# A two-layer hybrid encoder trunk: the order of the first loads, products and transposes

## Chip, cores and metric

The kernel runs on one core of one Trainium2 chip. The metric is the device time of one execution in microseconds; three runs of the kernel before are given by their median. Besides, one execution was profiled; all rows below come from it.

## Reference

The input `x` has 512 positions of 1024 features. Layer 0 mixes positions by windowed attention (16 query heads and 2 key and value heads of 64, chunks of 64 positions, a window of two chunks, a learned sink per head, key and query normalised over the head and partly rotated). Layer 1 mixes them by retention with 4 heads. Each layer then has a gated MLP with 2816 hidden features and a causal depthwise convolution of width 3. What the change touches is the beginning of layer 0:

```python
h = rmsnorm(x, norm1_g[0])
qkv = h @ w_qkv                      # 1024 -> 1024 queries, 128 keys, 128 values
q, k = rmsnorm(q, q_gain), rmsnorm(k, k_gain)   # over each head of 64
q, k = rotary(q), rotary(k)                     # first 16 of 64
p = softmax over the window and the sink of (q @ k.T) / 8
x = x + (p @ v) @ w_o
```

## The kernel before

Everything is float32 and is multiplied exactly enough by a split: each factor is a high part in fp32r and a rest, and a product is three matmuls (`mm3`, L1055: high by high, high by rest, rest by high). The input stands transposed in `x`, eight tiles of 128 features by 512 positions. ScalarE writes the high part of a weight or of a hidden tile (L287, L291), VectorE subtracts it to get the rest (L538, L543), and TensorE consumes both. Weights pass through two slots, `raw`, `w_hi` and `w_lo` with 2048 columns each. A pair of slots is a unit of work with a number (`PAIR_KV` 0, `PAIR_Q` 1 and 2, `PAIR_WO` 3 and 4, and so on); SyncE issues the load of a slot when VectorE has finished with its raw weights (`w_lo_ok`), ScalarE rewrites the high part when TensorE has finished with it (`w_used`), and TensorE waits for the rest (`unit`, L1067).

All five engines run programs that are written out by hand, each in a fixed order, and meet by semaphores. At the beginning:

- SyncE (L238) issues the first key and value load (four of the eight k, 1024 columns, slot 0), x tiles 0 to 4, the second load (slot 1), x tiles 5 to 7, and then the four query loads of 1 MB.
- ScalarE (L309 on) copies the first load in two halves, makes the high parts of x tiles 0 to 4, copies the second load, makes tiles 5 to 7, squares x tiles 0 to 3 (L302), copies the first query unit, squares tiles 4 to 7 and copies the second unit.
- VectorE (L557 on) follows it: two halves of the weights' rest, the hidden rests, the second load's rest behind tile 4; then it adds the squares up (L572, L575) with the first query unit's rest behind the third add; then the variance (L551) and the second unit's rest.
- TensorE (L1088 on) does for each of the two loads four position tiles with four k each, 128 by 256 columns: 96 matmuls into banks 0 to 3. Then come the four query units (`for cb ... for s`, L1139), each with four position tiles of 12 matmuls with 512 columns. Items are numbered n: 0 to 3 are the key and value tiles, 4 to 7 the tiles of the first 512 query columns (complete at the end of the second unit), 8 to 11 those of the rest. Ahead of tile 1 of the first unit, `columns` (L1070) multiplies the sum of squares by a column of ones into bank 6. Ahead of tile 2 it waits for the variance. Behind tile 2 of the second unit the two key heads are turned (`turn_in(0)`, `turn_in(1)`, L1101, transposes of the normalised and rotated keys). In the third unit, tiles 2 and 3 write over the banks of the turned keys and wait until these are copied out (`tp_ok`). Behind tile 0 of the fourth unit the first query heads are turned (`turn_in(2)` to `(5)`); that needs the rotations of items up to 7 (`qrot_ok` 8).
- An item passes through this chain: ScalarE squares it (`q_square`, L327, up to one item ahead of VectorE's sums), VectorE sums it over heads and scales (`q_var`), POOL takes the root (L933), VectorE normalises (L599), POOL rotates it in four steps (L945, L947, L949, L952) and copies keys (L955). ScalarE copies turned keys out in six pieces a head (`turned_out`, L335); it does this for head 0 behind the square of item 6, for head 1 behind that of item 7, and then copies the fourth query unit's weights. VectorE has that unit's rest between item 5's normalisation and item 7's sums, and the first output weights' rest behind item 7.
- POOL sets up constants, takes the root of the variance (L919) and serves the items, later the probabilities (L990).

The heads follow in a chain of their own over all four engines up to TensorE's first output product, and from there the kernel is the two MLPs and the retention, whose loops the change doesn't touch.

## Time and profile before

| what | us |
|---|---|
| median of three runs | 1292.45 (1292.0 to 1293.49) |
| the profiled execution | 1293.06 |
| its span, first to last instruction | 1291.2 |
| TensorE matmul, busy | 1269.8 |
| VectorE, busy | 697.9 |
| ScalarE, busy | 476.3 |
| POOL, busy | 202.0 |

The time of an execution is a little longer than the span of its instructions. In rows of a timeline the first number is the start in us from the start of the span, the second the length in us (of all, where x is over 1); then come engine, line of the kernel, operation, output and inputs with their sizes, the count, and in brackets how long the engine had been idle and who is taken to have ended that. TensorE's matmuls overlap, so the pace is the distance of their starts. The releaser is inferred, and where a wait is for several semaphores the name can be wrong: TensorE's first product is put down to a POOL clear, but waits also for the first hidden rest.

### The profile page before, as it was taken

The page shows a single profiled execution, that of the slowest core. Times are in us where ns is not written, and L with a number is a line of the kernel's source. Part 1 is how long each engine was busy: PE and PEld are TensorE (multiplying, and loading weights), DVE is VectorE, ACT ScalarE, POOL GpSimd, SP SyncE. Part 2 cuts the span into 40 slices and gives each one's busy share as a digit, 9 for nine tenths or more (in the row PEclk, how much of TensorE's full clock was granted, in tenths as well). Part 3 has the DMA queues.
Part 4 walks back from the last instruction along what each step waited for, and adds up shares of the span by engine and source line. Part 5 has one row for each costly group of instructions (what it writes and reads, how often), then busy time and mean ns, then how long its engine had stood idle before and what let it go on. Part 6 is the DMA issues. An engine that isn't in the chain of part 4 may idle for free.

```text
span 1291.2 us, 15660 instructions
## 1 busy us (share of the span) xinstructions
PE 1269.8 (98%) x5824; PEld 1051.7 (81%) x5824; DVE 697.9 (54%) x868; ACT 476.3 (37%) x663; POOL 202.0 (16%) x199
## 2 busy tenths in 40 slices
PE   7989999999999999999999999999999999999999
PEld 7856888888888888888888888888788888888887
DVE  5466456666665233535534644635666666664221
ACT  5566344444443222333223233223444444442111
POOL 4762300000000000402401501501700000000000
PEclk9999999999999999999999999999999999999999
DMA  6200222222222323421221221221122222222322
GB/s 235 89 15 34 98 98 97 97 97 97 97 77 68 111 91 112 153 90 65 98 98 65 97 95 61 82 86 65 65 98 97 97 97 97 97 77 90 105 97 88
DMA packets 19986, 118.79 MB, mean 92 GB/s; under 512 B 2448, under 2 KB 2448, under 8 KB 9072
## 3 DMA queue, kind: packets, MB, share of 16 engines
q1 hardware_dynamic: 19296, 116.40, 25.3%
q10 hardware_dynamic: 432, 1.59, 0.4%
q8 instruction: 21, 0.34, 0.1%
q0 software_dynamic: 224, 0.35, 0.1%
q14 instruction: 13, 0.11, 0.0%
HBM read 116.23 MB, written 2.10 MB: 92 GB/s over the span
## 4 chain that ended last, share of the span: by engine, by line
PE 91%; POOL 4%; issue 2%; DVE 1%; ACT 1%; DMA 0%; SPq 0%; POOLq 0%; ACTq 0%; DVEq 0%
PE ps L1057 30%; PE ps L1058 30%; PE ps L1059 30%; POOL qs L933 1%; POOL ssum L911 1%; POOL x L1036 1%; PE ps L1134 1%; PE ps L1074 1%; PE ps L1082 0%; POOL qn L990 0%; PE ps L1181 0%; ACT ex L377 0%; DMA x<-in_xT 0%; POOL ra L945 0%; POOL kd L952 0%
## 5 line engine op out<-in xcount | busy, mean ns | idle before, releaser
L1057 PE MATMUL ps<-h_hi,w_hi 128*128 128x512 f32 x960 | 375.9, 392 | 2.4 <-DVE h_lo L543 2.3
L1058 PE MATMUL ps<-h_lo,w_hi 128*128 128x512 f32 x960 | 374.0, 390 | 0.0
L1059 PE MATMUL ps<-h_hi,w_lo 128*128 128x512 f32 x960 | 374.0, 390 | 0.0
L538 DVE TENSOR_TENSOR w_lo<-raw,w_hi 128x2048 fp32r<-128x2048 f32 (+2 forms) x117 | 249.7, 2135 | 149.9 <-ACT w_hi L287 149.7
L287 ACT ACTIVATE w_hi<-raw 128x2048 fp32r<-128x2048 f32 (+2 forms) x117 | 205.5, 1757 | 236.0 <-PE ps L1059 235.1
L1057 PEld LDWEIGHTS ps<-h_hi,w_hi 128*128 128x128 f32 x960 | 180.5, 188 | 40.7 <-DVE h_lo L543 3.9
L1059 PEld LDWEIGHTS ps<-h_hi,w_lo 128*128 128x128 f32 x960 | 180.5, 188 | 37.9
L1058 PEld LDWEIGHTS ps<-h_lo,w_hi 128*128 128x128 f32 x960 | 180.6, 188 | 36.4
L1058 PE MATMUL ps<-g_lo,w_hi 128*128 128x512 f32 x352 | 136.9, 389 | 0.0
L1057 PE MATMUL ps<-g_hi,w_hi 128*128 128x512 f32 x352 | 136.9, 389 | 0.0
L1059 PE MATMUL ps<-g_hi,w_lo 128*128 128x512 f32 x352 | 136.9, 389 | 0.0
L428 ACT ACTIVATE y<-u,cvec 128x512 f32<-128x512 f32 x88 | 71.4, 816 | 141.4 <-DVE u L707 70.9
L1057 PE MATMUL ps<-w_hi,h_hi 128*128 128x512 f32 (+1 forms) x224 | 86.3, 385 | 7.1 <-POOL ve L894 6.9
L1058 PE MATMUL ps<-w_lo,h_hi 128*128 128x512 f32 (+1 forms) x224 | 85.1, 380 | 0.0
L1059 PE MATMUL ps<-w_hi,h_lo 128*128 128x512 f32 (+1 forms) x224 | 85.1, 380 | 0.0
L908 POOL TENSOR_TENSOR ssum<-sq 128x512 f32<-128x512 f32 x7 | 10.1, 1438 | 477.1 <-ACT sq L456 260.6
L1059 PEld LDWEIGHTS ps<-g_hi,w_lo 128*128 128x128 f32 x352 | 66.1, 188 | 13.8
L1058 PEld LDWEIGHTS ps<-g_lo,w_hi 128*128 128x128 f32 x352 | 66.1, 188 | 13.8
L1057 PEld LDWEIGHTS ps<-g_hi,w_hi 128*128 128x128 f32 x352 | 66.1, 188 | 13.5
L713 DVE SCALAR_TENSOR_TENSOR y<-u,cvec,y 128x512 f32<-128x512 f32 x88 | 65.6, 748 | 19.5 <-ACT y L428 19.5
L709 DVE TENSOR_TENSOR u<-ps,rbc 128x512 f32<-128x512 f32 x44 | 30.4, 690 | 77.9 <-PE ps L1059 77.9
L434 ACT ACTIVATE g_hi<-gp 128x512 f32 (+1 forms) x44 | 27.8, 632 | 118.3 <-DVE gp L722 118.3
(150 smaller groups left out, 1491.1 us busy)
## 6 DMA issues: line engine op xcount, KB each, us to landing
raw<-in_w_up SPq DMA_DIRECT2D x44, 1024.0 KB, 4.7
raw<-in_w_ret SPq DMA_DIRECT2D x32, 1024.0 KB, 4.8
raw<-in_w_dn SPq DMA_DIRECT2D x32, 704.0 KB, 4.0
raw<-in_w_q SPq DMA_DIRECT2D x4, 1024.0 KB, 4.9
raw<-in_w_ao SPq DMA_DIRECT2D x4, 1024.0 KB, 4.9
x<-in_xT SPq DMA_DIRECT2D x8, 256.0 KB, 5.8
out<-x SPq DMA_DIRECT2D x8, 256.0 KB, 5.2
raw<-in_w_kv SPq DMA_DIRECT2D x2, 512.0 KB, 5.3
```

The lines of the kernel that those rows point to most:

```text
L287: nc.scalar.activation(w_hi[:, s, 0:cols], raw[:, s, 0:cols], ACT.Copy).then_inc(w_hi_ok, 1)
L428: nc.scalar.activation(y[:, ab, :], u[:, ab, 2:S + 2], ACT.Identity, scale=c[:, 0:1], bias=c[:, 1:2]).then_inc(yb_ok, 1)
L434: nc.scalar.activation(g_hi[:, bass.ds(i, 1), :].rearrange("p o f -> p (o f)"), gp[:, :], ACT.Copy).then_inc(ghi_ok, 1)
L538: nc.vector.tensor_tensor(w_lo[:, s, 0:cols], raw[:, s, 0:cols], w_hi[:, s, 0:cols].bitcast(F32), ALU.subtract).then_inc(w_lo_ok, 1)
L709: nc.vector.tensor_tensor(u[:, 1, 2:S + 2], ps[:, 2 * s + 1, :], rbc[:, 0, :], ALU.mult).then_inc(u_ok, 1)
L713: nc.vector.scalar_tensor_tensor(y[:, ab, :], u[:, ab, 1:S + 1], c[:, 4 * ab + 1:4 * ab + 2], y[:, ab, :], ALU.mult, ALU.add).then_inc(y1_ ...
L911: nc.gpsimd.tensor_tensor(ssum[:, :], ssum[:, :], sq[:, m % 2, :], ALU.add).then_inc(ssum_ok, 1)
L933: nc.gpsimd.tensor_tensor(qs[:, n % 2, 0:heads], qvar[:, n % 2, 0:heads], mhalf[:, 0:heads], ALU.pow).then_inc(qs_ok, 1)
L1036: nc.gpsimd.tensor_tensor(x[:, m, :], x[:, m, :], rt[:, m % 4, :], ALU.add).then_inc(xe_ok, 1)
L1057: nc.tensor.matmul(dst, st[0], mv[0], start=start, stop=False)
L1058: nc.tensor.matmul(dst, st[0], mv[1], start=False, stop=False)
L1059: return nc.tensor.matmul(dst, st[1], mv[0], start=False, stop=stop)
```

## The change

The key and value weights become eight pieces of 256 columns, one for each k, all in slot 1; two of the pieces are issued by ScalarE's queue, the others by SyncE between the x tiles. The first query unit's weights get slot 0 from the start. ScalarE and VectorE handle one piece and one x tile in turn, and then the first query unit in two halves, ahead of all squares and adds. TensorE takes k as its outer loop. Ahead of the first piece it multiplies zeros, six times 256 columns into bank 6, from a square buffer that VectorE clears. The ones-products stand ahead of tile 2 in place of tile 1, in bank 7, and the wait for the variance ahead of tile 3. The keys are turned behind tile 3 in place of tile 2 of the second unit, and ScalarE copies both turned heads behind the square of item 7. Nothing computed changes but the order in which the keys' partial products are issued.

```diff
@@ -49,7 +49,10 @@
 KH = FT // 2
 UW = 2048
 DW = KH * P
-KVW = 4 * 256
+KVC = 256
+KV_ACT = 3
+WARM_COLS = 256
+WARM_MMS = 6
 PAIR_KV = 0
@@ -179,7 +182,9 @@
         r_in = sem("r_in")
         o_out = sem("o_out")
         warm_ok = sem("warm_ok")
-        w_half_ok = sem("w_half_ok")
+        zero_ok, pe_warm, q_half_ok = sem("zero_ok"), sem("pe_warm"), sem("q_half_ok")
+        kv_in = [sem(f"kv_in{k}") for k in range(KT)]
+        kv_hi_ok, kv_lo_ok = sem("kv_hi_ok"), sem("kv_lo_ok")
         cst = sem("cst")
         w_loaded = [sem("w_loaded0"), sem("w_loaded1")]
         w_hi_ok, w_lo_ok, w_used = sem("w_hi_ok"), sem("w_lo_ok"), sem("w_used")
@@ -234,22 +239,38 @@
         GROUPS = [(g // NCH, g % NCH) for g in range(A_KVH * NCH)]
+        def kv_cols(k):
+            return 1, slice(k * KVC, (k + 1) * KVC)
+
+        def kv_load(eng, k):
+            if k < KT:
+                s, cols = kv_cols(k)
+                landed = w_loaded[1] if k == KT - 1 else kv_in[k]
+                eng.dma_start(raw[:, s, cols], w_kv[:, cols]).then_inc(landed, 16)
+
+        def kv_wait(eng, part, unit_done, k):
+            if k % 4 == 3:
+                eng.wait_ge(unit_done, k // 4 + 1)
+            else:
+                eng.wait_ge(part, k - k // 4 + 1)
+
+
         @block.sync
         def _(sp):
-            def load(src, pair, s, cols, first=False):
-
-                if not first:
-                    sp.wait_ge(w_lo_ok, 2 * pair + s - 1)
+            def load(src, pair, s, cols):
+                sp.wait_ge(w_lo_ok, 2 * pair + s - 1)
                 sp.dma_start(raw[:, s, 0:cols], src).then_inc(w_loaded[s], 16)
-            load(w_kv[0], PAIR_KV, 0, KVW, first=True)
             for k in range(KT):
                 sp.dma_start(x[:, k, :], xT[k]).then_inc(x_in[k], 16)
-                if k == 4:
-                    load(w_kv[1], PAIR_KV, 1, KVW, first=True)
-            for cb in range(2):
-                for s in range(2):
-                    load(w_q[2 * cb + s], PAIR_Q + cb, s, UW)
+                if k == 0:
+                    kv_load(sp, 0)
+                if k + 1 >= KV_ACT:
+                    kv_load(sp, k + 1)
+            sp.dma_start(raw[:, 0, :], w_q[0]).then_inc(w_loaded[0], 16 * (PAIR_Q + 1))
+            load(w_q[1], PAIR_Q, 1, UW)
+            for s in range(2):
+                load(w_q[2 + s], PAIR_Q + 1, s, UW)
             for j in range(2):
                 for s in range(2):
                     load(w_ao[2 * j + s], PAIR_WO + j, s, UW)
@@ -279,11 +300,12 @@
         @block.scalar
         def _(act):
             act.dma_start(gain[:, :, :], gains).then_inc(g_in, 16)
-
-            def split(pair, s, cols, first=False):
+            for k in range(1, KV_ACT):
+                kv_load(act, k)
+
+            def split(pair, s, cols):
                 act.wait_ge(w_loaded[s], 16 * (pair + 1))
-                if not first:
-                    act.wait_ge(w_used, 2 * pair + s - 1)
+                act.wait_ge(w_used, 2 * pair + s - 1)
                 nc.scalar.activation(w_hi[:, s, 0:cols], raw[:, s, 0:cols], ACT.Copy).then_inc(w_hi_ok, 1)
             def hi_part(norm, m):
@@ -309,19 +331,24 @@
             act.wait_ge(warm_ok, 1)
             nc.scalar.activation(warm[:, :], warm[:, :], ACT.Copy)
-            act.wait_ge(w_loaded[0], 16)
-            nc.scalar.activation(w_hi[:, 0, 0:KVW // 2], raw[:, 0, 0:KVW // 2], ACT.Copy).then_inc(w_half_ok, 1)
-            nc.scalar.activation(w_hi[:, 0, KVW // 2:KVW], raw[:, 0, KVW // 2:KVW], ACT.Copy).then_inc(w_hi_ok, 1)
             act.wait_ge(g_in, 16)
             for k in range(KT):
-                act.wait_ge(x_in[k], 16)
-                hi_part(NORM_A, k)
-                if k == 4:
-                    split(PAIR_KV, 1, KVW, first=True)
+                s, cols = kv_cols(k)
+                if k == 0:
+                    act.wait_ge(x_in[k], 16)
+                    hi_part(NORM_A, k)
+                act.wait_ge(w_loaded[1] if k == KT - 1 else kv_in[k], 16)
+                nc.scalar.activation(w_hi[:, s, cols], raw[:, s, cols],
+                                     ACT.Copy).then_inc(w_hi_ok if k % 4 == 3 else kv_hi_ok, 1)
+                if k > 0:
+                    act.wait_ge(x_in[k], 16)
+                    hi_part(NORM_A, k)
+            act.wait_ge(w_loaded[0], 16 * (PAIR_Q + 1))
+            nc.scalar.activation(w_hi[:, 0, 0:UW // 2], raw[:, 0, 0:UW // 2], ACT.Copy).then_inc(q_half_ok, 1)
+            nc.scalar.activation(w_hi[:, 0, UW // 2:UW], raw[:, 0, UW // 2:UW], ACT.Copy).then_inc(w_hi_ok, 1)
+            act.wait_ge(pe_warm, 1)
             for k in range(KT):
                 square(SQ_BASE[NORM_A], k, x[:, k, :])
-                if k == 3:
-                    split(PAIR_Q, 0, UW)
             split(PAIR_Q, 1, UW)
             def q_square(n, width):
@@ -362,8 +389,8 @@
             act.wait_ge(c_in, 16 * C_DMAS)
             for n in range(4, 8):
                 q_square(n, S)
-                if n >= 6:
-                    turned_out(n - 6)
+            for g in range(2):
+                turned_out(g)
             split(PAIR_Q + 1, 1, UW)
             def exps(g):
@@ -555,16 +582,22 @@
                 nc.vector.tensor_tensor(x[:, m, :], ps[:, bank, :], x[:, m, :], ALU.add).then_inc(xe_ok, 1)
             nc.vector.memset(warm[:, :], 0.0).then_inc(warm_ok, 1)
-            dve.wait_ge(w_half_ok, 1)
-            nc.vector.tensor_tensor(w_lo[:, 0, 0:KVW // 2], raw[:, 0, 0:KVW // 2],
-                                    w_hi[:, 0, 0:KVW // 2].bitcast(F32), ALU.subtract)
-            dve.wait_ge(w_hi_ok, 1)
-            nc.vector.tensor_tensor(w_lo[:, 0, KVW // 2:KVW], raw[:, 0, KVW // 2:KVW],
-                                    w_hi[:, 0, KVW // 2:KVW].bitcast(F32), ALU.subtract).then_inc(w_lo_ok, 1)
+            nc.vector.memset(sq[:, 0, 0:WARM_COLS], 0.0).then_inc(zero_ok, 1)
             for k in range(KT):
-                lo_static(NORM_A, k)
-                if k == 4:
-                    split(PAIR_KV, 1, KVW)
+                s, cols = kv_cols(k)
+                if k == 0:
+                    lo_static(NORM_A, k)
+                kv_wait(dve, kv_hi_ok, w_hi_ok, k)
+                nc.vector.tensor_tensor(w_lo[:, s, cols], raw[:, s, cols], w_hi[:, s, cols].bitcast(F32),
+                                        ALU.subtract).then_inc(w_lo_ok if k % 4 == 3 else kv_lo_ok, 1)
+                if k > 0:
+                    lo_static(NORM_A, k)
+            dve.wait_ge(q_half_ok, 1)
+            nc.vector.tensor_tensor(w_lo[:, 0, 0:UW // 2], raw[:, 0, 0:UW // 2],
+                                    w_hi[:, 0, 0:UW // 2].bitcast(F32), ALU.subtract)
+            dve.wait_ge(w_hi_ok, 2 * PAIR_Q + 1)
+            nc.vector.tensor_tensor(w_lo[:, 0, UW // 2:UW], raw[:, 0, UW // 2:UW],
+                                    w_hi[:, 0, UW // 2:UW].bitcast(F32), ALU.subtract).then_inc(w_lo_ok, 1)
             for m in range(1, KT):
                 dve.wait_ge(sq_ok, SQ_BASE[NORM_A] + m + 1)
@@ -573,9 +606,7 @@
                 else:
                     dve.wait_ge(ssum_ok, SQ_BASE[NORM_A] + m)
                     nc.vector.tensor_tensor(ssum[:, :], ssum[:, :], sq[:, m % 2, :], ALU.add).then_inc(ssum_ok, 1)
-                if m == 3:
-                    split(PAIR_Q, 0, UW)
-            variance(ST_A, 0, D)
+            variance(ST_A, 0, D, bank=7)
             split(PAIR_Q, 1, UW)
             def q_var(n, heads):
@@ -1085,19 +1116,23 @@
                 last.then_inc(bc_done, 1)
+            pe.wait_ge(zero_ok, 1)
+            for _ in range(WARM_MMS):
+                last = nc.tensor.matmul(ps[:, 6, 0:WARM_COLS], sq[:, 0, 0:P], sq[:, 0, 0:WARM_COLS],
+                                        start=True, stop=True)
+            last.then_inc(pe_warm, 1)
             pe.wait_ge(cst, 1)
-            for s in range(2):
-                unit(PAIR_KV, s)
+            for k in range(KT):
+                s, cols = kv_cols(k)
+                kv_wait(pe, kv_lo_ok, w_lo_ok, k)
+                pe.wait_ge(h_ready, k + 1)
                 for t in range(PT):
-                    for k4 in range(4):
-                        k = 4 * s + k4
-                        if t == 0:
-                            pe.wait_ge(h_ready, k + 1)
-                        last = mm3(ps[:, t, 0:256], hidden(k, t * P, (t + 1) * P),
-                                   weights(s, k4 * 256, (k4 + 1) * 256), k == 0, k == KT - 1)
-                    if s == 1 and t < PT - 1:
+                    last = mm3(ps[:, t, 0:KVC], hidden(k, t * P, (t + 1) * P), (w_hi[:, s, cols], w_lo[:, s, cols]),
+                               k == 0, k == KT - 1)
+                    if k == KT - 1 and t < PT - 1:
                         last.then_inc(tile_done, 1)
-                last.then_inc(w_used, 1)
+                if k % 4 == 3:
+                    last.then_inc(w_used, 1)
             def turn_in(g):
                 if g < 2:
@@ -1141,9 +1176,9 @@
                     unit(PAIR_Q + cb, s)
                     for t in range(PT):
                         if cb == 0 and s == 0:
-                            if t == 1:
-                                columns(ST_A, SQ_BASE[NORM_A] + KT)
                             if t == 2:
+                                columns(ST_A, SQ_BASE[NORM_A] + KT, bank=7)
+                            if t == 3:
                                 pe.wait_ge(var_ok, ST_A + 1)
                         if cb == 1 and s == 0:
                             pe.wait_ge(v_ok, t + 1)
@@ -1165,7 +1200,7 @@
                                     turn_in(g)
                             else:
                                 scores(t - 1)
-                        if cb == 0 and s == 1 and t == 2:
+                        if cb == 0 and s == 1 and t == PT - 1:
                             pe.wait_ge(c_in, 16 * C_DMAS)
                             turn_in(0)
                             turn_in(1)
@@ -1420,7 +1455,7 @@
         return w.reshape(kt, P, n // per, per, P).transpose(2, 1, 3, 0, 4).reshape(n // per, P, per * kt * P)
     wqkv = A(attn_w_qkv)[0]
-    arrays["w_kv"] = c(moving(wqkv[:, D:], 256))
+    arrays["w_kv"] = c(moving(wqkv[:, D:], KVC).transpose(1, 0, 2).reshape(P, KT * KVC))
     arrays["w_q"] = c(np.concatenate([moving(wqkv[:, 0:S], S), moving(wqkv[:, S:D], S)]))
     arrays["w_ao"] = c(stationary(A(attn_w_o)[0], KT, 2))
     for layer in range(2):
```

## Rows read from the trace of the kernel before

**Rows 1.** The page's fourth part: the chain that ended last, by engine.
```profile
PE 91%; POOL 4%; issue 2%; DVE 1%; ACT 1%; DMA 0%; SPq 0%; POOLq 0%; ACTq 0%; DVEq 0%
```
**Rows 2.** TensorE's timeline: the first key product and the first query product.
```profile
6.93 0.55 PE L1057 MATMUL ps<-w_hi,h_hi 128*128 128x256 f32 x1 [6.93 <-POOL ve L894]
...
22.40 0.40 PE L1057 MATMUL ps<-w_hi,h_hi 128*128 128x512 f32 x1
```
**Rows 3.** Stretches: busy us (x count) by engine, granted clock, DMA share, GB/s.
```profile
9.50:14.50 5.00, 5.00 (x25) 5.00 (x25) 3.43 (x6) 4.09 (x7) 1.15 (x4) 1.00 1.07 409
14.50:22.40 7.90, 7.90 (x67) 7.90 (x66) 6.11 (x8) 4.98 (x7) 0.00 (x0) 1.00 0.38 136
...
0.00:10.10 10.10, 2.98 (x11) 2.52 (x12) 4.31 (x8) 6.11 (x9) 7.89 (x18) 1.00 0.82 277
...
0.00:14.60 14.60, 7.48 (x32) 7.02 (x33) 7.60 (x12) 9.83 (x15) 9.04 (x22) 1.00 0.90 319
76.00:79.50 3.50, 1.49 (x10) 1.04 (x11) 2.83 (x10) 3.06 (x16) 3.48 (x5) 1.00 0.00 0
79.50:83.00 3.50, 3.50 (x15) 2.01 (x14) 1.99 (x7) 1.44 (x6) 1.45 (x2) 0.51 0.02 5
```
**Rows 4.** TensorE's timeline: ones-products, first turning of queries, first output product.
```profile
25.15 0.95 PE L1074 MATMUL ps<-ones,ssum 128*128 128x1 f32 x8
...
59.64 1.94 PE L1115 MATMUL ps<-ident,qn 128*128 128x128 f32 x16
...
113.30 0.50 PE L1057 MATMUL ps<-a_hi,w_hi 128*128 128x512 f32 x1
```
**Rows 5.** POOL's timeline: an addition of the rotation twice, roots of items 7 and 9.
```profile
36.55 2.27 POOL L952 TENSOR_TENSOR kd<-ra,rb 128x32 f32<-128x32 f32 x1
...
40.01 0.25 POOL L952 TENSOR_TENSOR kd<-ra,rb 128x32 f32<-128x32 f32 x1
...
54.61 1.65 POOL L933 TENSOR_TENSOR qs<-qvar,mhalf 128x8 f32<-128x8 f32 x1 [4.71 <-DVE qvar L587]
...
59.03 0.46 POOL L952 TENSOR_TENSOR qn<-ra,rb 128x128 f32<-128x128 f32 x1
...
66.55 1.65 POOL L933 TENSOR_TENSOR qs<-qvar,mhalf 128x8 f32<-128x8 f32 x1
```
**Rows 6.** The chain that ended last, in order of time: two float32 score products.
```profile
86.10 0.86 PE ps L1134 x4
```
**Rows 7.** ScalarE's timeline: copies of weights, of turned keys, and item 7's square.
```profile
10.88 1.06 ACT L287 ACTIVATE w_hi<-raw 128x1024 fp32r<-128x1024 f32 x1 [0.91 <-DMA raw<-in_w_kv]
...
43.16 0.67 ACT L344 ACTIVATE kTo<-ps,gcol 64x512 f32<-64x512 f32 x1
...
46.19 0.69 ACT L332 ACTIVATE sqq<-ps,rcol 128x512 f32<-128x512 f32 x1 [0.33 <-PE ps L1059]
...
49.49 1.92 ACT L287 ACTIVATE w_hi<-raw 128x2048 fp32r<-128x2048 f32 x1
57.12 1.92 ACT L287 ACTIVATE w_hi<-raw 128x2048 fp32r<-128x2048 f32 x1 [5.71 <-PE ps L1059]
```
**Rows 8.** VectorE's timeline: weights' rests, adds of squares, item 9's variance.
```profile
11.97 1.23 DVE L538 TENSOR_TENSOR w_lo<-raw,w_hi 128x1024 fp32r<-128x1024 f32 x1 [1.21 <-ACT w_hi L287]
...
15.10 0.68 DVE L572 TENSOR_TENSOR ssum<-sq 128x512 f32<-128x512 f32 x1
16.48 1.49 DVE L575 TENSOR_TENSOR ssum<-ssum,sq 128x512 f32<-128x512 f32 x2 [0.70 <-ACT sq L302]
...
21.06 3.08 DVE L575 TENSOR_TENSOR ssum<-ssum,sq 128x512 f32<-128x512 f32 x4
...
36.42 2.29 DVE L538 TENSOR_TENSOR w_lo<-raw,w_hi 128x2048 fp32r<-128x2048 f32 x1
...
59.14 2.50 DVE L538 TENSOR_TENSOR w_lo<-raw,w_hi 128x2048 fp32r<-128x2048 f32 x1 [1.86 <-ACT w_hi L287]
...
65.81 0.27 DVE L587 TENSOR_SCALAR qvar<-qss 128x8 f32<-128x8 f32 x1
```

## The prediction

> **What bounds the kernel now.** I read the chain that ended last first: 91% of it is TensorE and 4% POOL [rows 1], so a change pays only where it lets TensorE start earlier, run faster or wait less, and where nothing behind it gives that back. Then I read TensorE's timeline at the start. Its first product starts at 6.93 us and the first query product at 22.40 [rows 2]. Between them the stretches count 25 products of 256 columns in 5.00 us up to 14.50, and 67 in 7.90 us behind it, edges included [rows 3]: one every 0.21 us, which is 1.2 GHz, and then one every 0.12 us, about 2.4 GHz, although the granted clock is shown as 1.00 for both. Ahead of the first change of clock the pace is to be read from the counts. All 96 key and value products would need 11.5 us at the fast pace, and take 15.5. So 6.9 us of idle time and 4 us lost to the slow pace stand ahead of the query products. From there TensorE is fed without a gap to the first turning of the queries at 59.64 [rows 4], and then it shares the chain with POOL, which computes roots, rotates and scales for the heads [rows 5].
>
> **Zero products.** Two float32 products of 256 columns take 0.86 us at full clock (four records) [rows 6], so six take 2.6 us, or 5.2 at half. They start behind a VectorE clear at about 1.3 us and end by 6.5. The first true product needs the first x tile, the gain and a piece of 256 columns: less work than today's halves of 512, so 6.3 to 6.9 instead of 6.93. I take 6.5: the zero products hide behind the loads.
>
> **Key and value products.** Piece by piece TensorE needs 12 products, 1.44 us at the fast pace, while VectorE needs about 1.0 us for each k (0.66 and a third) and ScalarE as much; the x tiles arrive at 1 us each or so. I add 0.4 for early gaps: 6.5 + 11.5 + 0.4 = 18.4 instead of 22.4, if the clock is up. That is the 4 us the change could win.
>
> **First query unit.** It now has a slot of its own, so its load is issued without a wait. Ahead of its last byte lie 1.05 MB of key and value weights, 2.10 of x and 0.36 of constants; with its own 1.05 that makes 4.56 MB, and today 319 GB/s for 14.60 us are 4.66 MB [rows 3]. So the data is in by 14.3 to 14.6. The second key and value load shows the lag: 2.72 MB stand up to its end, 277 GB/s for 10.10 us are 2.80 MB, and ScalarE gets it at 10.88 [rows 3, 7]. Lag 0.9, so 15.2 us. The pieces have packets of 1 KB where the loads now have 4 KB; no row has the price. Bounds: nothing, and twice the time for that MB, 3.3 us at the mean rate. I take 0.5, near to nothing, because the x tiles' 2 KB packets stand in the same mean: 15.7. Two half copies and two half subtractions, of 1.06 and 1.23 us at 1024 columns [rows 7, 8], overlapped, take 3.45: ready at 19.15. TensorE is through the keys by 18.4 and waits 0.7 here.
>
> **Squares, and the columns moved by one tile.** VectorE can add squares only behind these subtractions. The first add to the second takes 1.38, the rest 0.80 each [rows 8]: seven adds end 6.1 us later, at 25.2. The ones-products now stand ahead of the third tile, 19.2 + 5.45 = 24.7; they wait for the sum until 25.3. Today they start at 25.15 [rows 4]. So all that follows from the variance (root, keys' norms) is where it was, and TensorE is one tile ahead, 2.7 us. As the sum sets this point, the key products may end as late as 19.8 for nothing. From 25.3: 0.8 for the ones-products, two tiles (5.44; one took 2.75 from 22.40 to the ones-products at 25.15, 2.72 without its first step), one unit (10.88) gives 42.4 for the end of the fourth tile of the second unit. Today ScalarE squares this tile at 46.19 [rows 7]; now at 42.6, 3.6 earlier, 0.8 of it because the keys are not yet turned.
>
> **Keys turned behind the fourth tile: a new wait.** Today ScalarE copies the first keys out at 43.16, ahead of the fourth tile's square, and only the second batch (2.72 us) lies behind it, to the copy at 49.49 [rows 7]. Now both batches lie behind: 42.6 + 0.58 + 2.70 + 2.72 = 48.6 for that copy, only 0.9 earlier than today. Queued behind it are VectorE's subtraction, the variance of query tile 7, POOL's root (5.12 us behind the copy, at 54.61 today [rows 5, 7]) and the last two rotations, whose end is 4.88 behind the root's start (59.49). The root comes at 53.7, the end at 58.6 at the earliest. But TensorE, 2.9 ahead even with the keys' turning of 0.8 added, is ready to turn the queries at 56.7 and needs both rotations.
>
> Nor does POOL get through unhindered. A POOL addition of 0.25 us took 2.27 when it started 0.13 behind a VectorE subtraction of 2048 columns, and ended with it [rows 5, 8]. The subtraction for the output weights starts 2.02 behind its copy (57.12 to 59.14), and this copy hangs on TensorE's third unit, so it now comes at 54.3 and the subtraction from 56.3 to 58.6. Today it starts when the last rotation has begun [rows 5, 8]; now one and a half rotations are ahead of POOL. What is left takes 1.55 to 2.16 behind 58.6: POOL is done at 60.2 to 60.8, and TensorE turns the queries at about 60.5 instead of 59.64, having stood still for 3.8 us. The lead is gone, and 0.9 more. By the Trainium skill, "SBUF — State Buffer", section "SBUF: two separate sides", the port pair of these two engines is an exclusive lock and goes to the one that starts first; by that rule the outcome hangs on which of two starts 0.1 us apart is first, and the range of 0.6 above is that question. The trace agrees: the subtraction at 59.14, begun while POOL ran, took 2.50 where others take 2.29.
>
> **Sum.** The next root (query tile 9) starts at 66.55, when POOL comes free; its input was there at 66.08 [rows 5, 8]. With TensorE 0.9 later the input comes at 67.0, so the heads start 0.4 later. Clock: with TensorE busy for 1.49 of 3.50 us up to 79.50, the granted clock of the next 3.50 us was 0.51 [rows 3]. A stand of 3.8 us is at least as idle. Bounds: 0, and 1.7 for such a fall over busy time. I take 0.6, since part of the slow stretch lies in the stand itself. Total +1.0 on the profiled execution: span 1291.2 to 1292.2, time 1293.06 to 1294.1. It stands 0.6 over the median of the three runs, 1292.45, so against the median I expect 1293.5.
>
> **Rivals.** A measurement of this kernel can tell about 0.2%, 2.6 us, from no change.
> (a) The lead gets through. If POOL is not held up and rotates by 58.6, TensorE's input for tile 9 is ready 1 us sooner than today, worth 1.0 to 1.5; if also the loads come earlier or the rotations' order lets TensorE keep what it has at the query units, up to 2.9 us: 1289.6. For it: TensorE really is ahead there. Against: the addition of 2.27 us, and two batches of copies on ScalarE ahead of the rotations. The part up to 1.5 faster: 0.14; the part near 2.9: 0.15.
> (b) The zero products do not raise the clock, so the change doesn't do what it says. Then the key products run at 0.21 for the first 7.5 us again and end at about 21.3; the ones-products come at 26.8, everything behind 1.5 later than in my sum: +2.5, 1295.0. Nothing in the trace shows zero data. Chance 0.08.
> (c) Slower: the clock falls in the stand at the queries' turning and stays low through the turning (1.7) and tile 1 (2.8), which lead to POOL's root of tile 9. It decides from when the slow stretch covers over 4 us of this busy time at full pace; two stretches as long as that of the trace would do so and cost 3.4, +3.8, 1296.2. Chance 0.12. The Trainium skill, "TensorE: Matmul & The Clock Gate", section "What's actually happening", says that half clock is the default and only activity releases it; by this rule the stand would bring a fall for certain, which with the 1.7 of the bound gives 1294.6. The trace agrees so far that the clock fell behind a mostly idle stretch and came back in a busy one.
>
> **How the numbers follow.** The forecast, a stand that takes the lead back with a short fall of the clock or none: 0.51, from 1292 to 1295. It, the small part of (a) and most of (b) are within 2.6 us: 0.67. Faster by more is the large part of (a) and a little over: 0.17. Slower by more: (c) with the rest of (b) and of late loads: 0.16. The range leaves out about 1 in 10 on either side: 1289.7 to 1295.9.
>
> **What would show it.** Zero products from 1.3 us, true ones from 6.5 at a pace of 0.12; query unit 1 at 19.2, ones-products at 25.3 next to a last add at 25.2; ScalarE's fourth square at 42.6 and its copy at 48.6; a POOL addition or product of over 2 us near 56.3; TensorE idle for some 3.8 us up to 60.5; after it the granted clock 0.5 or 1.0. The forecast is wrong if TensorE turns the queries before 58.5, if the key products are still at 0.21 behind 10 us, or if the attention ends more than 2.6 us before 113.30 [rows 4].

## The result, and the profile after

The changed kernel takes 1296.92 us in the median of 6 runs (1295.81 to 1297.31). The kernel before, run beside it, takes 1292.22 (6 runs, 1290.47 to 1293.91). The ratio is 1.0034, with a 95% interval from 1.0024 to 1.0044: slower by 4.7 us. The profiled execution took 1296.81, against 1293.06 before, so 3.75 of the 4.7 us can be looked for in the two traces; the rest is scatter between executions.

The page's first lines and the chain by engine, beside [rows 1]: everything looks as before, only that TensorE is busy for 3.9 us more (1273.7 against 1269.8). The page does not say where, so the timeline has to be read.

```profile
span 1295.0 us, 15708 instructions
...
PE 1273.7 (98%) x5836; PEld 1053.9 (81%) x5836; DVE 698.4 (54%) x875; ACT 477.7 (37%) x669; POOL 204.5 (16%) x199
...
PE 90%; POOL 4%; issue 2%; DVE 1%; ACT 1%; DMA 1%; SPq 1%; POOLq 0%; DVEq 0%
```

TensorE's timeline of the changed kernel (start, us, and what the engine waited for ahead of it), beside [rows 2, 4]:

```profile
1.23 4.89 PE L1121 MATMUL ps<-sq 128*128 128x256 f32 x12 [1.23 <-DVE sq L585]
6.65 0.36 PE L1088 MATMUL ps<-w_hi,h_hi 128*128 128x256 f32 x1 [0.53 <-issue]
...
19.91 0.50 PE L1088 MATMUL ps<-w_hi,h_hi 128*128 128x512 f32 x1 [0.85 <-DVE w_lo L599]
...
25.88 1.05 PE L1105 MATMUL ps<-ones,ssum 128*128 128x1 f32 x8 [0.24 <-DVE ssum L608]
...
43.23 1.03 PE L1150 MATMUL ps<-ident,kd 128*128 128x128 f32 x8
...
61.47 3.65 PE L1150 MATMUL ps<-ident,qn 128*128 128x128 f32 x16 [3.46 <-POOL qn L983]
...
116.47 0.50 PE L1088 MATMUL ps<-a_hi,w_hi 128*128 128x512 f32 x1
```

The first query product comes 2.5 us earlier than before, the ones-products 0.7 later, the turning of the queries 1.8 later, and there TensorE stood still for 3.46 us. The same 16 products that took 1.94 us before [rows 4] take 3.65. The stretches of the changed kernel (columns as in [rows 3]) show why:

```profile
9.50:14.50 5.00, 4.99 (x42) 4.82 (x41) 4.02 (x8) 4.55 (x9) 1.79 (x4) 1.00 1.08 399
...
57.90:61.40 3.50, 0.11 (x1) 0.00 (x0) 2.88 (x3) 0.69 (x1) 3.40 (x5) 0.80 0.16 23
61.40:64.90 3.50, 3.43 (x17) 3.46 (x17) 0.75 (x1) 1.97 (x3) 2.56 (x5) 0.50 0.66 276
64.90:68.40 3.50, 3.50 (x14) 2.82 (x13) 0.00 (x0) 0.78 (x2) 0.43 (x1) 0.72 0.00 0
```

In the first, 42 products stand where 25 stood [rows 3]: the zero products do raise the clock, one product every 0.12 us from the start. In the others the granted clock falls inside the stand (0.80 of its stretch) and is at 0.50, which is 1.2 GHz, through the whole turning and about 2 us into the tile behind it. Counted from the three stretches, the slow clock lasts some 6.9 us, of which 1.4 lie in the stand; in the fall of [rows 3] it was half as long. The fall in the heads at 79.5 to 83 us [rows 3] is gone: from 70.0 to 113.3 the clock of the changed kernel is 1.00 throughout.

Another fall lies far behind the attention, near 930 us, between the retention and the second MLP, where the change touches nothing. First the changed kernel, then `e8_both` (an experiment below), one of three traces without it (the others are `e4_no_zeros` and `e5_rest_later`):

```profile
932.00:936.00 4.00, 3.08 (x8) 2.22 (x9) 1.81 (x3) 3.29 (x4) 3.71 (x3) 0.73 0.02 4
```

```profile
932.00:936.00 4.00, 4.00 (x21) 3.33 (x19) 2.20 (x1) 0.00 (x0) 0.09 (x2) 1.00 0.18 27
```

From the first output product to the end of the span it is 1178.5 us in the changed kernel and 1177.9 in the profiled execution before, which both have this fall, and 1177.0 in each of the three traces without it. So whole times can differ by 1.5 us for a reason that lies outside the change.

ScalarE, VectorE and POOL around that stand, beside [rows 5, 7, 8] (one timeline each):

```profile
43.43 0.69 ACT L359 ACTIVATE sqq<-ps,rcol 128x512 f32<-128x512 f32 x1 [2.03 <-PE ps L1090]
...
49.48 1.92 ACT L309 ACTIVATE w_hi<-raw 128x2048 fp32r<-128x2048 f32 x1
55.38 1.92 ACT L309 ACTIVATE w_hi<-raw 128x2048 fp32r<-128x2048 f32 x1 [3.99 <-PE ps L1090]
...
68.76 0.69 ACT L359 ACTIVATE sqq<-ps,rcol 128x512 f32<-128x512 f32 x1 [2.92 <-PE ps L1090]
```

```profile
57.40 2.53 DVE L565 TENSOR_TENSOR w_lo<-raw,w_hi 128x2048 fp32r<-128x2048 f32 x1
```

```profile
54.60 1.65 POOL L964 TENSOR_TENSOR qs<-qvar,mhalf 128x8 f32<-128x8 f32 x1 [3.79 <-DVE qvar L618]
...
57.92 2.31 POOL L976 TENSOR_TENSOR ra<-qn,rotg 128x128 f32<-128x128 f32 x1
...
60.87 0.45 POOL L983 TENSOR_TENSOR qn<-ra,rb 128x128 f32<-128x128 f32 x1
...
70.45 1.65 POOL L964 TENSOR_TENSOR qs<-qvar,mhalf 128x8 f32<-128x8 f32 x1 [5.12 <-DVE qvar L618]
```

Item 7's square is 2.8 us earlier than before, but the weights' copy behind it (49.48) and with it the root (54.60) are where they were, since both batches of keys are copied in between. VectorE's subtraction for the output weights starts at 57.40, and POOL's first product of the last rotation, 0.47 us elsewhere, takes 2.31. TensorE has been ready since about 58.0.

### The profile page after: what moved, and what is told of

The parts are those of the page before. It is cut to its first block, busy times and chain, and to the rows that moved or that the text cites. A ratio compares the mean times of both kernels' runs of the same rounds, so it can differ in the third digit from the quotient of the medians.

```text
span 1295.0 us, 15708 instructions
## 1 busy us (share of the span) xinstructions
PE 1273.7 (98%) x5836; PEld 1053.9 (81%) x5836; DVE 698.4 (54%) x875; ACT 477.7 (37%) x669; POOL 204.5 (16%) x199
## 4 chain that ended last, share of the span: by engine, by line
PE 90%; POOL 4%; issue 2%; DVE 1%; ACT 1%; DMA 1%; SPq 1%; POOLq 0%; DVEq 0%
PE ps L1088 29%; PE ps L1090 29%; PE ps L1089 29%; POOL qs L964 1%; DMA raw<-in_w_q 1%; POOL ssum L942 1%; POOL x L1067 1%; PE ps L1105 1%; PE ps L1169 1%; PE ps L1113 0%; POOL qn L1021 0%; PE ps L1216 0%; POOL ra L976 0%; ACT ex L404 0%; POOL rb L980 0%
## 5 line engine op out<-in xcount | busy, mean ns | idle before, releaser
L565 DVE TENSOR_TENSOR w_lo<-raw,w_hi 128x2048 fp32r<-128x2048 f32 (+1 forms) x115 | 246.2, 2141 | 145.0 <-ACT w_hi L309 144.9
L309 ACT ACTIVATE w_hi<-raw 128x2048 fp32r<-128x2048 f32 (+1 forms) x115 | 202.5, 1761 | 230.6 <-PE ps L1090 230.6
```

The lines of the kernel that those rows point to most:

```text
L309: nc.scalar.activation(w_hi[:, s, 0:cols], raw[:, s, 0:cols], ACT.Copy).then_inc(w_hi_ok, 1)
L565: nc.vector.tensor_tensor(w_lo[:, s, 0:cols], raw[:, s, 0:cols], w_hi[:, s, 0:cols].bitcast(F32), ALU.subtract).then_inc(w_lo_ok, 1)
```

## The experiments

Four questions were open: is it the place of the keys that costs; is it the clock, and what makes it fall; how much is VectorE's hold on POOL; and why does the beginning bring nothing. Ratios are to runs of the kernel before on the same chip in the same series (26, 24, 27 and 15 runs). Where a median is set beside that of the changed kernel, the two come from different chips; the ratios give the same differences to within half a microsecond.

**First series: the places of the keys, the stand, and the zeros.** `e1_keys_back` is the changed kernel with the keys turned where they were:

```diff
-                        if cb == 0 and s == 1 and t == PT - 1:    # TensorE
+                        if cb == 0 and s == 1 and t == 2:
...
                 q_square(n, S)                                    # ScalarE
-            for g in range(2):
-                turned_out(g)
+                if n >= 6:
+                    turned_out(n - 6)
```

> The changed kernel with the keys turned behind tile 2 again and the first head copied out behind item 6's square. Theory (the loss is made by both batches of key copies lying behind item 7's square): ScalarE's copy for the fourth query unit comes at about 48.0 instead of 49.5, POOL has rotated item 7 by 58.0, ahead of VectorE's subtraction, TensorE waits up to 1 us for the keys but not at the turning of the queries (58.7 instead of 61.5), the granted clock stays at 1.0 there: about 1291.2 us, 5.5 below the changed kernel and 1 below the kernel before. Rival (the pieces and the loads are what costs): within 1 us of the changed kernel, 1296.9.

Measured: 1292.49 us (10 runs), 1.0003 (0.9994 to 1.0013), 1.3 above the theory's number and far from the rival's. The loss is gone, 4.4 us of it in the medians, 4.0 by the ratios. TensorE's timeline has the turning at 59.08 and without a wait:

```profile
59.08 1.94 PE L1150 MATMUL ps<-ident,qn 128*128 128x128 f32 x16
```

It gains nothing on the kernel before: the turning is 0.56 earlier, and a fall of the clock in the heads came back (0.83 and 0.69 in the stretches from 76.0 and 79.5), so that the first output product starts at 113.42.

`e2_filled_stand` leaves the keys where the change put them and lets TensorE work in the stand. The products' result is overwritten by the turning:

```diff
                             if t == 0:
+                                pe.wait_ge(qn_ok, 5)
+                                for _ in range(14):
+                                    nc.tensor.matmul(ps[:, 4, :], h_hi[:, 0, 0:P], h_hi[:, 0, :],
+                                                     start=True, stop=True)
                                 for g in range(2, 6):
```

> The changed kernel with 14 products of 512 columns of hidden tile 0 ahead of the turning of the queries, into a free bank, 3.2 us of work in a stand of 3.5. Theory (the clock falls in the stand and costs 2.6 us in the turning and in tile 1): the turning starts at 61.5 as before, takes 1.7 instead of 3.3 us, tile 1 ends at 66.0 instead of 68.6, granted clock 1.0: 1294.3 us. Rival (POOL's chain sets the heads whatever TensorE does): 1296.9.

Measured: 1294.45 (10 runs), 1.0016 (1.0006 to 1.0025), as expected. TensorE's and ScalarE's timelines:

```profile
57.96 3.33 PE L1201 MATMUL ps<-h_hi 128*128 128x512 f32 x14
61.59 0.63 PE L1150 MATMUL ps<-ident,qn 128*128 128x128 f32 x4 [0.30 <-POOL qn L983]
```

```profile
66.32 0.69 ACT L359 ACTIVATE sqq<-ps,rcol 128x512 f32<-128x512 f32 x1 [1.64 <-PE ps L1090]
```

The turning starts at the same place as in the changed kernel (61.59 against 61.47), but from there to item 9's square it is 4.73 us, as in the kernel before (4.72), where the changed kernel takes 7.29. The clock is 1.00 there in this run. These 2.6 us are the half clock, since only the 14 products differ. In the medians it is 2.5 of the 4.7. What stays is the later turning.

`e3_zeros_alone` puts the clear, the six zero products and ScalarE's wait for them into the kernel before (TensorE's part is shown):

```diff
+            pe.wait_ge(zero_ok, 1)
+            for _ in range(6):
+                last = nc.tensor.matmul(ps[:, 6, 0:256], sq[:, 0, 0:P], sq[:, 0, 0:256],
+                                        start=True, stop=True)
+            last.then_inc(pe_warm, 1)
```

> The kernel before with the six zero products alone. Theory: the key products run at 0.12 us from the start and end at about 20 instead of 22.4, but the first query unit is ready at 21.1 as before and the sum of squares at 24.2, so TensorE and all behind it are 0.9 ahead: 1291.3 us. Rival (the whole 2.4 us gets through): 1289.8. Rival (nothing gets through, the heads are set by POOL): 1292.2.

Measured: 1292.26 (10 runs), 0.9997 (0.9988 to 1.0007). Its first query product is 1.0 us earlier than before (21.37, with a wait of 0.83 for the weights' rest), the ones-products 0.8, the first output product 1.4 (111.89). Half of those 1.4 us is that this trace has no fall of the clock in the heads. In the median it is the rival's number (nothing gets through), and the third series shows that the beginning without zeros can be as early in a single trace.

`e4_no_zeros` is the changed kernel without them (their clear and the waits for them are gone too):

```diff
-            for _ in range(WARM_MMS):
-                last = nc.tensor.matmul(ps[:, 6, 0:WARM_COLS], sq[:, 0, 0:P], sq[:, 0, 0:WARM_COLS],
-                                        start=True, stop=True)
```

> The changed kernel without the zero products. Theory: the key products run at 0.21 us to about 14 us and end at 21.3 instead of 19.1, the ones-products stand at 26.8 instead of 25.9, and all behind is 0.9 later, with the stand at the queries as before: 1297.8 us. Rival (the zero products are what costs, by the clock or by holding up the first piece): 1294 or less. Rival (the sum of squares sets the point alone): 1296.9.

Measured: 1297.13 (5 runs, 1294.11 to 1298.15), 1.0036 (1.0022 to 1.0050). For the whole kernel the zeros are worth nothing that can be told here; in the traces they are worth 0.3 us at the turning. The execution that was profiled is the one of 1294.11 us, and it teaches more than the median. TensorE's timeline and two stretches:

```profile
61.76 1.94 PE L1143 MATMUL ps<-ident,qn 128*128 128x128 f32 x16 [3.41 <-POOL qn L981]
```

```profile
58.30:61.80 3.50, 0.09 (x2) 0.07 (x2) 2.77 (x3) 0.69 (x1) 3.42 (x5) 1.00 0.09 14
61.80:65.30 3.50, 3.50 (x24) 3.20 (x25) 0.75 (x1) 2.42 (x4) 2.56 (x5) 1.00 0.71 286
```

The same stand, TensorE busy for 0.09 of 3.50 us, and no fall. Item 9's square comes 4.72 behind the turning, as in the filled kernel. So a stand makes the fall possible and doesn't bring it each time. The 2.57 us between 4.72 and 7.29 are the price read a second time. That this execution is 3.2 us below the median of the other four isn't a third reading: it also lacks the fall near 930 us, and has one in the heads.

**Second series: VectorE's hold on POOL, who carries the place of the keys, and the loads.** `e5_rest_later` moves VectorE's subtraction for the output weights behind item 8's norm:

```diff
-            split(PAIR_WO, 0, UW)
             q_var(8, 8)
             q_norm(8, 8)
+            split(PAIR_WO, 0, UW)
```

> The changed kernel with VectorE's subtraction for the first output weights moved behind item 8's normalisation. Theory (this subtraction holds POOL up in item 7's rotation): the root starts at 54.6 as before, the rotations end 4.9 later at 59.5 instead of 61.3, TensorE stands 1.7 instead of 3.5 us and turns the queries at 59.6; a stand that short leaves the granted clock at 1.0, so tile 1 ends at 64.2 instead of 68.6: about 1292.0 us, 5 below the changed kernel. Rival (the key copies alone make the stand, the subtraction costs nothing): queries turned at 61.4, 1296.9.

Measured: 1293.09 (10 runs), 1.0003 (0.9994 to 1.0013). POOL's timeline, then TensorE's:

```profile
58.08 0.45 POOL L974 TENSOR_TENSOR ra<-qn,rotg 128x128 f32<-128x128 f32 x1
...
62.51 2.44 POOL L974 TENSOR_TENSOR ra<-qn,rotg 128x128 f32<-128x128 f32 x1 [0.86 <-DVE qn L630]
```

```profile
59.76 1.94 PE L1148 MATMUL ps<-ident,qn 128*128 128x128 f32 x16 [1.56 <-POOL qn L981]
```

The root is where it was (54.75), the product takes 0.45, the turning comes 1.7 earlier and the stand is 1.56; the clock did not fall there. The moved subtraction holds POOL up again, at 62.51, where no one waits for it. Of the 4.7 us, 3.8 in the medians (4.0 by the ratios) hang on the place of this one subtraction, through the length of the stand and the clock together. As undoing the keys' move took back as much, it takes both to make the loss.

`e6_tensor_order` takes back only TensorE's half of the keys' move (the first of the two edits of `e1_keys_back`). ScalarE still copies both batches behind item 7's square.

> The changed kernel with the keys turned behind tile 2 on TensorE, but ScalarE's order left: both heads copied behind item 7's square. Theory (ScalarE's order makes the copy late): TensorE waits 1 us for the keys, squares item 7 at 44.4 and starts the copy for the fourth unit at 50.4, 0.9 later than the changed kernel; the queries are turned at 62.4: 1296 to 1298 us. Rival (TensorE's place alone matters): like e1_keys_back, 1292.5.

Measured: 1299.46 (4 runs), 1.0051 (1.0034 to 1.0068), the slowest of all, above what was expected. TensorE's timeline, then ScalarE's:

```profile
63.61 3.65 PE L1150 MATMUL ps<-ident,qn 128*128 128x128 f32 x16 [3.44 <-POOL qn L983]
```

```profile
45.56 0.69 ACT L359 ACTIVATE sqq<-ps,rcol 128x512 f32<-128x512 f32 x1 [4.13 <-PE ps L1090]
...
51.61 1.92 ACT L309 ACTIVATE w_hi<-raw 128x2048 fp32r<-128x2048 f32 x1
```

TensorE waits 1.0 for POOL's keys, the square is 2.1 later, and both batches still stand between it and the weights. It is the order on ScalarE that decides, and with the turning behind tile 2 it must be the order of before.

`e7_two_loads` asks why the first query unit's weights came at 16.40 and not at 15.7: key and value weights by two DMAs of 1024 columns in place of eight of 256, so with packets of 4 KB:

```diff
-            if k < KT:
-                s, cols = kv_cols(k)
+            if k % 4 == 0 and k < KT:
+                s, cols = 1, slice(k * KVC, (k + 4) * KVC)
```

> The changed kernel with the key and value weights loaded by two transfers of 1024 columns (packets of 4 KB) in place of eight of 256; copies and products stay in eight pieces. Theory (the small packets cost 1.2 us): the first query unit's weights are there at 15.2 instead of 16.4, ones-products at 24.7 instead of 25.9, queries turned at 60.3 instead of 61.5, the stand as long as before with its fall of the clock: 1295.7 us. Rival (the place in SyncE's queue, not the packets, makes them late): weights at 16.4, 1296.9.

A miss: 1297.05 (9 runs), 1.0034 (1.0024 to 1.0044), and ScalarE's timeline has the weights no earlier:

```profile
16.58 1.06 ACT L347 ACTIVATE w_hi<-raw 128x1024 fp32r<-128x1024 f32 x1 [0.98 <-DMA raw<-in_w_q]
```

Packets of 1 KB were not the price, nor were the two loads on ScalarE's queue, which this run has not. Up to 14.6 us the changed kernel moves 289 GB/s where the kernel before moves 319 [rows 3]. `e7_two_loads` moves 293, and `e3_zeros_alone`, which has the zero products with the loads of before, 317. So the lower rate comes with the new order of the loads; what in it costs that stays open.

`e8_both` is `e1_keys_back` and `e7_two_loads` together.

> The changed kernel with the keys' order of before (as e1_keys_back) and the two loads (as e7_two_loads). Theory: 1.2 us ahead of e1_keys_back through all of the beginning, queries turned at 57.9 without a stand: about 1291.0 us, 1 below the kernel before. Rival (a lead at the queries is lost in POOL's chain of the heads): 1292.3.

Measured: 1292.13 (10 runs), 0.9995 (0.9986 to 1.0005), the rival's number: the turning is at 59.14 and not at 57.9, as in `e1_keys_back`. Its trace has the shortest span of all (1289.1, first output product at 112.08), 2.9 us below that of `e1_keys_back`, but by the clock: 1.4 us because it stays at 1.00 in the heads, and 1.6 because it stays at 1.00 near 930 us. In the medians it can't be told from before.

**Third series: does the clock in the heads matter?** In `e9_both_filled`, `e10_before_filled` and `e11_zeros_filled`, TensorE does products of 256 columns ahead of its waits in the heads (5 ahead of four turnings of probabilities, 8, 4 and 2 ahead of the first three groups' values), into banks that are overwritten. They are built on `e8_both`, the kernel before, and `e3_zeros_alone`. The wait for `alo_ok` ahead of the values is moved up with them, ahead of the added products:

```diff
+            def fill(bank, n):
+                for _ in range(n):
+                    nc.tensor.matmul(ps[:, bank, 0:256], h_hi[:, 0, 0:P], h_hi[:, 0, 0:256],
+                                     start=True, stop=True)
...
+                fill(probs_bank(g), 5 if 1 <= g <= 4 else 0)
                 pe.wait_ge(pn_ok, g + 1)
```

> e8_both with products of 256 columns on hidden tile 0 in TensorE's waits of the first heads (five ahead of four turnings of probabilities, eight, four and two ahead of the first three value products; 0.12 us each, into banks that are free). Theory (the scatter of some 3 to 4 us of all kernels here, and the lead that e8_both does not show in its median, are falls of the clock in the first heads, 79 to 83 us): no fall there, the stretch from the turning of the queries to the first output product always near 52.9 us, runs at the low end of e8_both: 1291.0 us, 0.1% below the kernel before. Rival (the scatter comes from elsewhere): 1292.2 or, with the added products in the way, more.

> The kernel before with the same added products in the first heads. Theory: as for e9_both_filled, the fall of the clock at 79.5 us goes, the first output product comes 0.8 us sooner (112.5): 1291.4 us. Rival: 1292.3 or more.

> e3_zeros_alone with the same added products in the first heads. Theory: the 0.7 us that it led at the queries and the heads without a fall add up, first output product at 111.9: 1290.9 us. Rival (nothing adds up): 1292.2.

All three miss: 1293.39, 1293.72 and 1293.32 (11 runs each), with 1.0007 (0.9998 to 1.0016), 1.0009 (0.9999 to 1.0018) and 1.0008 (0.9999 to 1.0017). The clock is at 1.00 from 55 to 112 us in all three, and from the turning of the queries to the first output product each takes 54.12 us. `e8_both`, without filling and without a fall, takes 52.94, and the kernel before, with its fall, 53.66. So filling costs 1.2 us, more than the 0.7 of the fall that it prevents. Nor does it end the scatter between executions: all three still spread over 3 us, and all three traces have the fall near 930 us.

The beginnings of the three show one thing more, in the stretch from 10.00 to 13.30 us; first the kernel before with filled heads, whose beginning is that of the kernel before, then `e11_zeros_filled`:

```profile
10.00:13.30 3.30, 3.30 (x24) 3.30 (x23) 2.00 (x3) 2.79 (x4) 1.16 (x4) 1.00 1.06 423
```

```profile
10.00:13.30 3.30, 2.80 (x13) 2.80 (x14) 1.98 (x4) 2.26 (x4) 1.67 (x4) 0.51 1.06 411
```

The kernel before has 18 products in this stretch in the execution shown at the top, and 24 here, with the same instructions: the clock rose earlier by itself. What follows in that trace is earlier as well:

```profile
23.77 1.05 PE L1074 MATMUL ps<-ones,ssum 128*128 128x1 f32 x8
...
58.42 1.94 PE L1115 MATMUL ps<-ident,qn 128*128 128x128 f32 x16
```

The ones-products come 1.4 us earlier than in the execution at the top and the turning of the queries 1.2, without any change to the beginning. And behind the zero products it can fall again: in `e11_zeros_filled` TensorE waited 2.4 us for the activations' rests, and what followed ran at half pace. Its ones-products come at 25.46, later than the 25.15 of before; the other execution of this beginning, in `e3_zeros_alone`, had them at 24.36.

**Last run: is there a version that beats both?** `e12_squares_first` is `e8_both` with the first two squares on ScalarE, and their addition on VectorE, ahead of the first query unit's weights, in the gap in which both wait for them:

```diff
+            act.wait_ge(pe_warm, 1)
+            for k in range(2):
+                square(SQ_BASE[NORM_A], k, x[:, k, :])
             act.wait_ge(w_loaded[0], 16 * (PAIR_Q + 1))
...
+            dve.wait_ge(sq_ok, SQ_BASE[NORM_A] + 2)
+            nc.vector.tensor_tensor(ssum[:, :], sq[:, 0, :], sq[:, 1, :], ALU.add).then_inc(ssum_ok, 2)
             dve.wait_ge(q_half_ok, 1)
```

> e8_both with the first two squares and their add put ahead of the first query unit's copies, into the 1 to 1.7 us in which ScalarE and VectorE wait for its load. Theory (the adds behind the unit's subtractions set the ones-products): the last add ends 1.3 us sooner, TensorE reaches the ones-products without a wait at 25.5 instead of 26.0, everything to the turning of the queries 0.5 ahead (58.6): 1291.7 us, which cannot be told from the kernel before. Rival (the load of the unit alone sets the point): 26.0 as before, 1292.1.

Measured: 1291.95 (11 runs, 1290.07 to 1293.4) against 1293.29 (15 runs), 0.9988 (0.9979 to 0.9997). TensorE's timeline:

```profile
25.48 0.95 PE L1109 MATMUL ps<-ones,ssum 128*128 128x1 f32 x8
...
58.51 1.94 PE L1154 MATMUL ps<-ident,qn 128*128 128x128 f32 x16
...
111.47 0.50 PE L1092 MATMUL ps<-a_hi,w_hi 128*128 128x512 f32 x1
```

The sum no longer sets the ones-products. The turning comes 1.1 us earlier than in the execution of before that is shown at the top, but no earlier than in that of `e10_before_filled` (58.42), which has the same beginning as before. The interval lies just under 1: it beats the changed kernel clearly and the kernel before by about 0.12%, which is less than the 0.2% that single comparisons can tell.

## Why the prediction was wrong, and where it was right

It expected 1293.5 us, the same as before, and a range up to 1295.9. The measured 1296.92 lies outside. The path up to the stand was right; the term of the sum that failed is the clock's.

**Right: the mechanism up to the stand.** The zero products hid behind the loads and raised the clock (6.65 for 6.5, one product each 0.12 us). The ones-products waited for the sum. Both batches of keys went between item 7's square and the copy (6.05 us from one to the other; the prediction had 6.0), which held the root where it was. The output weights' subtraction held POOL up for 1.84 us, and TensorE stood still for 3.46 (3.8 predicted; TensorE, too, came to it later than forecast, at 58.0 and not 56.7). Undoing the keys' move took the whole loss back (`e1_keys_back`), and moving the subtraction took back the turning's delay (`e5_rest_later`).

**Failed: the clock's term.** "I take 0.6, since part of the slow stretch lies in the stand itself." The bounds were 0 and 1.7, from a fall over busy time as long as that of [rows 3]. Measured it is 2.57: the turning and the tile behind it take 7.29 us to item 9's square, against 4.72 in the kernel before and 4.73 with the stand filled. Part of the slow stretch did lie in the stand, but the stretch was twice as long as that of [rows 3], so that 2.57 of the 4.72 us of work ran at half pace. That was rival (c), with its place, its mechanism and its two lengths, at a chance of 0.12. Its price of 3.4 leaves out the part in the stand, and the slow stretch did not cover the over 4 us of full-pace work that it asked for; two lengths give 3.4, which is not over 4, so that rival's own sum didn't meet its condition. The upper bound of 1.7 came from one fall in one trace and was taken for the length that every fall has. In `e7_two_loads` the fall was of that length and cost 1.6 (6.36 us from the turning to the square), in `e6_tensor_order` 2.8 (7.54). The sentence on the rule that only activity releases the clock, by which a stand brings a fall for certain, is not borne out as a certainty: the changed kernel, `e6_tensor_order` and `e7_two_loads` fell, `e4_no_zeros` in its profiled execution did not. Yet its 1294.6 was nearer than mine. The Trainium skill, "TensorE: Matmul & The Clock Gate", section "What's actually happening", says of the rise that the watch on activity runs on its own and doesn't start with the kernel, so that its point varies from run to run; the two executions of one beginning, with 18 and 24 products (`e10_before_filled`), agree, and a fall that comes in one execution and not in another would follow from the same.

**Too small: the landing of the first query unit's weights.** "I take 0.5, near to nothing": they were ready for ScalarE at 16.40 and not 15.7, and this 0.7 went through the sum (ones-products 25.88, not 25.3), the square (43.43, not 42.6), the copy (49.48, not 48.6) and the root (54.60, not 53.7) to the turning (61.47, not 60.5). The reason given, packets of 1 KB, was wrong as well (`e7_two_loads`); the slower mean rate was not foreseen at all.

**The sum, mended.** Turning 1.83 later (0.86 predicted) and 2.57 of half clock make 4.4 at item 9's square. The next root starts at 70.45 instead of 66.55, so 3.9 later: before, it had to wait half a microsecond for POOL [rows 5, 8]. The attention ends 3.17 later, since the fall of the clock in the heads did not come this time. The span is 3.8 longer, as the fall near 930 us, which the change doesn't touch, took 0.6 more in this execution than in the one before. The remaining 0.9 between the profiled difference and the medians' 4.7 is the execution that was profiled before, 0.8 over the 1292.22 of its comparison.

**Why the beginning brings nothing.** Even without the stand, 2.4 us of lead at the first query product (19.96 for 22.40) are 0.56 at the turning of the queries (`e1_keys_back`: 59.08 for 59.64). The lead is spent at the waits for the sum of squares and for POOL's keys (1.00 in that run), which hang on ScalarE, VectorE and POOL and not on TensorE. When the squares were moved too, the turning came at 58.51. But the trace of before is one execution, in which the clock rose late; with an early rise the same beginning turns the queries at 58.42 (`e10_before_filled`), ahead of all the changed ones. So the traces show no lead of a changed beginning at that point that is larger than the 1.2 us by which two executions of the old one differ. The forecast, which measured everything from the one late trace, could not see this.

## What to carry to other kernels

When a step is moved on the engine that bounds the kernel, follow it on the engine that drains it: here the turning takes TensorE 0.8 us at either place, and the copies that it brought onto ScalarE, both ahead of the weights for the norm behind them, cost the time. A stand of TensorE of some three microseconds should be priced at its own length plus a fall of the clock over the work behind it, up to the next wait for another engine; here that fall cost nothing once and 1.6, 2.6 and 2.8 us otherwise, so the whole span belongs in the range with a chance. Before a difference of a microsecond between two traces is read as the change, their granted clocks should be compared everywhere, in the parts that the change doesn't touch too. Two microseconds won at the start are worth what the next sum, root or rotation lets through, so look for the engine that these hang on before the products.

## What the runs showed of the hardware

- How idle a stretch is doesn't settle whether the clock falls. TensorE busy for 0.11, 0.17 and 0.24 us of a stretch of 3.50 brought a fall in the changed kernel, `e6_tensor_order` and `e7_two_loads`; 0.09 in `e4_no_zeros` brought none. In the heads 1.39 of 3.50 us brought none in the changed kernel (79.5 to 83) and 1.97 none in `e8_both`, and 2.02 did in `e1_keys_back`. A single trace can't price it. The mean granted clock of each execution is on record: 0.996 or 0.997 in all six of the changed kernel, 0.995 to 0.997 in all four of `e6_tensor_order`, all nine of `e7_two_loads` and four of the five of `e4_no_zeros`, whose profiled one has 0.999. That fits a fall in the stand in all but one of them; the mean doesn't say where a fall lay.
- Most of the scatter of a kernel is such falls. The ten executions of `e1_keys_back` took 1290.96 and 1291.02 us at a mean clock of 1.000, 1292.08 to 1292.59 at 0.999 and 1293.87 to 1294.32 at 0.997.
- The slow stretch differs in what it covers: the turning took 3.65 us in the changed kernel and `e6_tensor_order` and 2.79 in `e7_two_loads`, after the same stand. In the first two the clock had fallen inside the stand (0.80 and 0.88 of its 3.50 us), in the third not before the turning (1.00, then 0.65).
- Six float32 products of zeros raise the clock for real products that follow at once (one each 0.12 us from the first on, where `e4_no_zeros` starts at 0.21; 42 in 5 us, where kernels without zeros had 25, 33 and 36), but it is lost again when TensorE then waits (`e11_zeros_filled`), and it sometimes rises early without them (`e10_before_filled`).
- A VectorE subtraction of 2048 columns and POOL's products excluded each other as a whole: 0.45 us of POOL took 2.31 and 2.44 behind a subtraction of 2048 columns, and the subtraction took 2.53 instead of 2.29 when POOL was in first.
- Filling the waits of TensorE with products is not free even when it waits anyway: 34 products of 256 columns in the heads cost 1.2 us and saved 0.7.
